# A transformer stack in split fp32 on one Trainium2 core: order of the latent fronts, the network rows, the first tiles and the mixed layer's entry, two bank placements, and bias reads spread over eight weight units

## The chip, the cores and the metric

The kernel runs on one core of one Trainium2 chip. The metric is the device time of one execution in microseconds (us), lower is better. Engines are called by the profile's names: PE (TensorE; PEld its weight loads), DVE (VectorE), ACT (ScalarE), POOL (GpSimd) and SP (SyncE, which here only issues DMAs). PSUM is eight banks of 128 partitions by 512 fp32 numbers.

## The reference, cut to what matters

512 tokens of width 1024 go through a first block of four layers (latent attention "mla", windowed attention "swa", forget-gate attention "fox", and mla again), and then through a second block of one layer with four mixers, a gated feed-forward network and a gated addition:

```python
for i in range(4):                       # mla, swa, fox, mla
    y = branch_i(x)
    x = layernorm(8 ** 0.25 * x + y, ln_g[i], ln_b[i])

def mla(x):                              # each branch ends with w_out
    cq, ckv, k_rope, gate = split(x @ w_in, 384, 256, 32, 1024)
    q = rmsnorm(cq) @ w_q_up             # 16 heads of 64 + 32 rotated
    k, v = split(rmsnorm(ckv) @ w_kv_up)
    return (causal_attention(q, k, v) * silu(gate)) @ w_out

h = rmsnorm(x); z = h @ w_in_2           # the second block, once
mix = concat(conv(z), pool(z), topk_attention(z, rel_bias), block_attention(z, rel_bias))
x = x + rmsnorm(mix @ w_out_2)
g, u = split(rmsnorm(x) @ w_gate_up)     # 2 x 2816 columns
x = x + rmsnorm((silu(g) * u) @ w_down)
x = x + sigmoid(rmsnorm(x) @ w_ple_gate) * (p @ w_ple_proj)
```

## The kernel before

**Weights.** Everything is a matrix product in split fp32: each operand is a high and a low part, and a product is three matmuls (`three`, lines 471 to 473). All weights pass in `units` of at most 128x1024 numbers (512 KB) in one fixed order (`plan_units`). For unit u, SP reads it into `w_raw` (ring of 3, line 1258) once the low part of unit u-3 is made; ACT copies it to `w_hi` (`split`, line 1277; ring of 4, so it also waits until PE has done with unit u-4); POOL subtracts to make `w_lo` (line 2604); PE waits for that in `unit`. ACT issues the splits at fixed places of its own program: `advance` splits the unit three ahead, and `early` pulls that next split forward to an earlier place.

**Products.** A `tile` is one unit of 128 columns against all 512 tokens: 8 steps of three matmuls, 24 in all, into one bank. Groups of results go in turn to banks 6 and 7; `begin` waits until the group before last of the same parity and all older ones have been drained (`bank_free`), unless the dictionary `place` names another bank, in which case it waits for nothing. `open_half` runs a unit against token columns 256 to 511 alone (24 matmuls of half the width) and leaves the group open for a later `tile` to finish; the third and fourth half opened at a time go to banks 4 and 5. `groups_stored(eng, n)` waits for all groups up to n.

**Token tiles.** `ROWS` is (3, 2, 1, 0). To multiply by x it must lie transposed: `turn_tile` on PE (8 transposes, line 871, into banks 2t and 2t+1), `turned_tile` on ACT (two copies to XTh, line 1498) and `low` on DVE (two subtractions to XTl, line 2161).

**Start.** SP reads the identity, four token tiles (line 1232) and then weights; PE transposes tiles 0 to 3; ACT copies all eight halves and then splits three units; PE then runs four whole tiles `c`.

**Latent fronts.** `mla` (used twice, j = 0 and 1) computes five latent tiles `c`, the sums of their squares, a rotated key tile and two gate tiles. On ACT `root` takes the square root of each sum and five copies make the high parts (line 1618). On DVE `scaled` takes a reciprocal of 128x512 (line 2250), scales (line 2252), and `low_latent` makes the low parts (line 2257). The three latents of the queries use the first root, the two of keys and values the second. After both, DVE finishes the two gate tiles (`gate`, line 1953), whose tanh ACT makes at line 1341. PE goes on with `rope(0)`, `query(0)`, `keys(0)`, whose groups follow the gates in banks 6 and 7.

**Row products.** `out_rows` multiplies n units of rows into all eight banks, four token tiles at a time; the last four units are held and run tile by tile in the order `ROWS`, with transposes of finished tiles put in at places given by `TURNS`: (row index, unit index) to which turn. `chunk_at(k)` gives the group count that unit k's input needs. The two calls for w_down have none and wait for every group first. `rms_tail` on ACT and DVE is the norm behind it: ACT squares, DVE adds and norms (`h_norm`, line 2175), each tile in a chain between the two. `ple_early` then runs the units of w_ple_gate on the first two rows between the last turns. `layer_tail_normed` and `ln_tail(3)` do the same after the last mla layer, where `early_mixed` opens four halves (`ik` and three `iq`) before the last two turns.

**Mixed layer's entry.** The halves are closed; PE transposes the small matrix of index weights (line 1095) as a group of its own, runs a fourth `iq` tile, and then goes through six pairs of a score block (line 1113) and a `conv` tile. The bias tables of the relative attention come back from DRAM to `G` as 32 reads of 64 KB (`bias_rows`, line 1239), four per head; SP issues two heads' reads ahead of each of the weight reads of four units from the first `conv` unit on, the first after waiting for `xt_lo`, the low parts of all turned tiles.

## Time and profile before

| | us |
|---|---|
| median of 3 runs | 1819.64 |
| lowest, highest | 1814.38, 1822.32 |
| the profiled execution | 1813.09 |
| its span | 1811.1 |
| PE busy | 1700.9 |
| DVE busy | 770.4 |
| ACT busy | 771.1 |
| POOL busy | 606.6 |

The time between span and the execution's own time is 1.99 us. Busy times of PE count a matmul's modelled end, so neighbours overlap a little. The rows further down are lines of the timeline, with the start and the duration in us from the span's start, and in square brackets the engine's idle time before the line and what ended it; and lines of the table by windows, with PE's busy time, the granted share of its full clock (1.00 is 2.4 GHz, 0.50 is 1.2 GHz), the DMA share and GB/s.

### The profile page before, as it was taken

The numbers are of one execution on the slowest core, as the hardware profiler recorded it, in microseconds if no ns is written. First come the engines' busy times: TensorE is split into PE (matmuls) and PEld (weight loads), VectorE is DVE, ScalarE is ACT, GpSimd is POOL, SyncE is SP. The second block draws the span as 40 slices with busy tenths as digits, with TensorE's granted clock in tenths as the row PEclk, the third lists the DMA queues.
The fourth block names the chain that finished last, engine by engine and source line by source line (L and its number), as shares of the span: only waits on it lengthen the run. The fifth ranks groups of instructions, "written<-read, shape, count | busy, mean of one in ns | idle before, by whom it ended". The sixth has DMA issues, their size and how long they took to land.

```text
span 1811.1 us, 24157 instructions
## 1 busy us (share of the span) xinstructions
PE 1700.9 (94%) x9303; PEld 1371.5 (76%) x9303; DVE 770.4 (43%) x2029; ACT 771.1 (43%) x1565; POOL 606.6 (33%) x304
## 2 busy tenths in 40 slices
PE   7899999999999999999899997997899999999988
PEld 6677778777788787787677777776678888787776
DVE  1566627456344434354565534877423111000152
ACT  4455643456244444433455633325634232112242
POOL 4222223323243332242422233372225444344323
PEclk9999999999999999999999998998899999999999
DMA  6221134233453222152321146321133333233312
GB/s 159 60 45 45 59 128 133 78 69 66 144 147 82 71 59 71 47 184 65 69 49 52 48 147 175 82 75 53 48 128 105 93 100 98 93 94 94 115 48 82
DMA packets 215693, 161.16 MB, mean 89 GB/s; under 512 B 53723, under 2 KB 196859, under 8 KB 215580
## 3 DMA queue, kind: packets, MB, share of 16 engines
q1 hardware_dynamic: 205616, 130.21, 25.6%
q10 hardware_dynamic: 9660, 29.12, 5.1%
q8 instruction: 75, 1.23, 0.3%
q0 software_dynamic: 304, 0.29, 0.2%
q14 instruction: 38, 0.31, 0.1%
HBM read 148.32 MB, written 11.14 MB: 88 GB/s over the span
## 4 chain that ended last, share of the span: by engine, by line
PE 61%; DVE 9%; ACT 5%; POOL 2%; DMA 2%; issue 2%; ACTq 1%; SPq 0%; POOLq 0%; DVEq 0%
PE banks L471 17%; PE banks L473 16%; PE banks L472 16%; PE banks L713 3%; PE banks L728 3%; PE banks L682 3%; POOL w_lo L2604 2%; ACT AB L1408 1%; ACT w_hi L1277 1%; DVE misc L2451 1%; DVE misc L2438 1%; PE banks L871 1%; DVE top L2450 1%; DVE AB L2101 1%; DVE QKl L1916 1%
## 5 line engine op out<-in xcount | busy, mean ns | idle before, releaser
L2604 POOL TENSOR_TENSOR w_lo<-w_raw,w_hi 128x1024 fp32r<-128x1024 f32 (+4 forms) x254 | 578.0, 2282 | 1174.9 <-ACT w_hi L1277 1174.6
L471 PE MATMUL banks<-XTh,w_hi 128*128 128x512 f32 (+3 forms) x1184 | 448.2, 379 | 23.3 <-POOL w_lo L2604 7.5
L473 PE MATMUL banks<-XTh,w_lo 128*128 128x512 f32 (+3 forms) x1184 | 441.8, 373 | 0.0
L472 PE MATMUL banks<-XTl,w_hi 128*128 128x512 f32 (+3 forms) x1184 | 441.5, 373 | 0.0
L1277 ACT ACTIVATE w_hi<-w_raw 128x1024 fp32r<-128x1024 f32 (+4 forms) x254 | 254.0, 1006 | 170.8 <-PE banks L473 90.7
L471 PEld LDWEIGHTS banks<-XTh,w_hi 128*128 128x128 f32 (+1 forms) x1184 | 224.0, 189 | 69.6 <-issue 22.0
L473 PEld LDWEIGHTS banks<-XTh,w_lo 128*128 128x128 f32 (+1 forms) x1184 | 223.8, 189 | 39.9
L472 PEld LDWEIGHTS banks<-XTl,w_hi 128*128 128x128 f32 (+1 forms) x1184 | 224.4, 190 | 38.3 <-issue 0.5
L471 PE MATMUL banks<-w_hi,OTh 128*128 128x512 f32 (+1 forms) x448 | 172.8, 386 | 6.8 <-POOL w_lo L2604 6.2
L473 PE MATMUL banks<-w_hi,OTl 128*128 128x512 f32 (+1 forms) x448 | 168.0, 375 | 0.0
L472 PE MATMUL banks<-w_lo,OTh 128*128 128x512 f32 (+1 forms) x448 | 167.8, 374 | 0.0
L1434 ACT ACTIVATE AB<-banks 128x512 f32<-128x512 f32 (+1 forms) x200 | 98.9, 528 | 147.3 <-PE banks L713 144.7
L1408 ACT ACTIVATE AB<-AB,nb 128x256 f32<-128x256 f32 (+3 forms) x288 | 152.9, 539 | 20.0 <-DVE nb L2082 17.1
L2529 DVE TENSOR_TENSOR otmp<-banks,AB 128x512 f32<-128x512 f32 x22 | 15.2, 692 | 280.9 <-PE banks L473 280.9
L2072 DVE CUSTOM_DVE_ANT_0 AB<-banks,zmask 128x384 f32<-128x384 f32 (+1 forms) x192 | 83.9, 487 | 102.1 <-PE banks L713 99.7
L2101 DVE TENSOR_SCALAR_CACHE_REDUCE AB<-AB,ri 128x256 f32<-128x256 f32 (+3 forms) x256 | 118.2, 518 | 2.3
L1916 DVE TENSOR_TENSOR QKl<-banks,QKh 128x512 fp32r<-128x512 f32 (+2 forms) x80 | 53.9, 682 | 135.4 <-ACT QKh L1307 134.2
L713 PE MATMUL banks<-ident,AB 128*128 128x128 f32 x672 | 98.0, 281 | 8.7 <-ACT AB L1434 5.9
L471 PEld LDWEIGHTS banks<-w_hi,OTh 128*128 128x128 f32 x448 | 84.3, 188 | 27.6 <-POOL w_lo L2604 8.3
L471 PE MATMUL banks<-w_hi,XTh 128*128 128x256 f32 (+2 forms) x288 | 90.7, 315 | 6.4 <-POOL w_lo L2604 5.6
L473 PEld LDWEIGHTS banks<-w_hi,OTl 128*128 128x128 f32 x448 | 84.3, 188 | 15.4
L713 PEld LDWEIGHTS banks<-ident,AB 128*128 128x128 f32 x672 | 73.7, 141 | 29.1 <-issue 17.5
(196 smaller groups left out, 2384.6 us busy)
## 6 DMA issues: line engine op xcount, KB each, us to landing
w_raw<-in_w_gate_up_dram SPq DMA_DIRECT2D x44, 512.0 KB, 3.8
w_raw<-in_fox_w_in_dram SPq DMA_DIRECT2D x30, 512.0 KB, 4.1
w_raw<-in_mla_w_in_dram SPq DMA_DIRECT2D x26, 512.0 KB, 4.1
w_raw<-in_w_in_dram SPq DMA_DIRECT2D x24, 512.0 KB, 3.8
w_raw<-in_w_down_dram SPq DMA_DIRECT2D x22, 512.0 KB, 3.5
w_raw<-in_swa_w_in_dram SPq DMA_DIRECT2D x20, 512.0 KB, 3.9
w_raw<-in_mla_w_out_dram SPq DMA_DIRECT2D x16, 512.0 KB, 3.6
x_spill<-AB ACTq DMA_DIRECT2D x16, 512.0 KB, 3.4
```

Source lines behind the costliest of these rows:

```text
L471: nc.tensor.matmul(o, ah, bh, start=first, stop=False, skip_group_check=True)
L472: nc.tensor.matmul(o, ah, bl, start=False, stop=False, skip_group_check=True)
L473: return nc.tensor.matmul(o, al, bh, start=False, stop=last, skip_group_check=True)
L682: mm = nc.tensor.matmul(bank[2 * (c.sch % 2) + x][:, cols], qp[r, pr.q, ts], kp[r, pr.k, ks], start=n == 0 and t == pr.s_chunks[ch][0], st ...
L713: mm = nc.tensor.transpose(bank[4 + c.tch % 2][:, o:o + P], SBP[a % 2][x][:, col:col + P], ident[:, :])
L1277: nc.scalar.activation(view(w_hi, u, RING), view(w_raw, u, RAW), ACT.Copy).then_inc(hi_done, 1)
L1408: ins = nc.scalar.activation(sc, sc, ACT.Exp, bias=nb[:, b, n0 + t:n0 + t + 1], scale=pr.scale, accum_out=rs[:, b, n0 + t:n0 + t + 1])
L1434: nc.scalar.activation(PTP[x][:, pr.pt[js[0]]:pr.pt[js[0]] + width], bank[4 + c.tch % 2][:, 0:width], ACT.Copy).then_inc(pt_free, 1)
L1916: return nc.vector.tensor_tensor(dst, src, h.bitcast(F32), ALU.subtract)
L2072: ins = nc.vector.tensor_tensor_reduce(pr.score(b, x, t), o, pr.bias(t, x), 1.0, -3e38, ALU.add, ALU.max, mx[:, b, 4 * x + t:4 * x + t + 1])
L2101: ins = nc.vector.tensor_scalar(pr.score(b, x, t), pr.score(b, x, t), ri[:, b, 4 * x + t:4 * x + t + 1], None, ALU.mult, ALU.add, accum_ou ...
L2604: pool.tensor_tensor(view(w_lo, u, RING), view(w_raw, u, RAW), view(w_hi, u, RING).bitcast(F32), ALU.subtract).then_inc(lo_done, 1)
```

## The change

It has these parts.

1. **First tiles.** SP reads token tiles 3 and 2, then two weight units, then token tiles 1 and 0, then the third unit. PE transposes tiles 3 and 2, opens the half of the first `c`, transposes tile 1, opens the second half, transposes tile 0, opens the third, and closes the three later. ACT copies tiles 3 and 2, splits unit 0, copies tile 1, splits unit 1, copies tile 0, splits unit 2. DVE follows in the same order.
2. **Latent fronts** (both mla layers). On ACT the high copies of the last two latents go behind the two gates' tanh. On DVE the first gate goes ahead of the second reciprocal and the second gate between it and the scaling.
3. **Network rows.** w_down's units wait each for its own group; the wait for all groups moves to the fourth token tile of the first unit. `TURNS["rms"]` turns the first finished tile one unit (six matmuls) later, in the two places where it is used, behind w_out_2 and behind w_down.
4. **Splits pulled forward.** In `rms_tail` `early()` goes between the last two copies; in `layer_tail_normed` ahead of the third and fourth deviation.
5. **Two groups in other banks.** The transposed index weights and the fourth `iq` tile go to banks 2 and 3, so that they wait for no `bank_free`.
6. **Bias reads.** One head's four reads go behind each of eight weight reads in place of eight ahead of each of four; the wait for `xt_lo` goes behind the first `conv` unit's read.

```diff
@@ -63,7 +63,7 @@
...
 ROWS = (3, 2, 1, 0)
-TURNS = {"ln": {(1, 3): 0, (2, 3): 1, (3, 3): 2}, "rms": {(2, 1): 0, (3, 1): 1}, "ln_rms": {(3, 1): 0, (3, 2): 1}}
+TURNS = {"ln": {(1, 3): 0, (2, 3): 1, (3, 3): 2}, "rms": {(2, 2): 0, (3, 1): 1}, "ln_rms": {(3, 1): 0, (3, 2): 1}}
 MLA_OUT = [5, 6, 7, 3, 4, 0, 1, 2]
@@ -809,7 +809,7 @@
...
                 paired = bool(begun)
-                if not begun:
+                if not begun and not chunk_at:
                     groups_stored(pe, c.g)
@@ -824,7 +824,7 @@
...
                             pe.wait_ge(pt_free, c.tch)
-                        if paired and k == 0 and t == T - 1:
+                        if (paired or chunk_at) and k == 0 and t == T - 1:
                             groups_stored(pe, c.g)
@@ -984,8 +984,18 @@
...
             pe.wait_ge(ident_in, 16)
-            for t in range(T):
-                turn_tile(t, lambda t: x_tok[:, t, :], (x_in[t], 16))
+
+            def turn_start(n):
+                turn_tile(ROWS[n], lambda t: x_tok[:, t, :], (x_in[ROWS[n]], 16))
+
+            turn_start(0)
+            turn_start(1)
+            pe.wait_ge(xt_lo, 4)
+            open_half("c")
+            turn_start(2)
+            open_half("c")
+            turn_start(3)
+            open_half("c")
             pe.wait_ge(xt_lo, c.xt)
@@ -1089,6 +1099,7 @@
...
                 tile("iq", n0=P)
+            place[c.g], place[c.g + 1] = 2, 3
             o = begin()
@@ -1169,13 +1180,15 @@
...
+            ff_at = []
             for lo, hi in ((0, KF_A), (KF_A, KF)):
...
                     tile("ff_up")
+                    ff_at.append(c.g)
                 out_rows("down", hi - lo, lambda k, ts: (ff_dst[lo + k][0][:, ff_dst[lo + k][2], ts],
                                                          ff_dst[lo + k][1][:, ff_dst[lo + k][2], ts]),
-                         first=lo == 0, last=lo > 0, turned=lambda t: HT[t % 2], turn_at=TURNS["rms"], early=ple_early)
+                         first=lo == 0, last=lo > 0, turned=lambda t: HT[t % 2], turn_at=TURNS["rms"], chunk_at=lambda k: ff_at[lo + k], early=ple_early)
                 if lo == 0:
@@ -1228,8 +1241,12 @@
...
             sp.dma_start(ident[:, :], consts["ident"]).then_inc(ident_in, 16)
-            for t in range(T):
+
+            def tokens(t):
                 sp.dma_start(x_tok[:, t, :], w["x"][0, t * P:(t + 1) * P, :]).then_inc(x_in[t], 16)
+
+            tokens(ROWS[0])
+            tokens(ROWS[1])
             conv0 = next(u for u, x in enumerate(units) if x[0] == "conv")
@@ -1241,12 +1258,9 @@
...
                     sp.wait_ge(lo_done, u - RAW + 1)
-                if u == conv0:
-                    sp.wait_ge(rel_dma, 16 * 8)
-                    sp.wait_ge(xt_lo, mark["mixed"])
-                if conv0 <= u < conv0 + 4:
-                    bias_rows(2 * (u - conv0))
-                    bias_rows(2 * (u - conv0) + 1)
+                if u == 2:
+                    tokens(ROWS[2])
+                    tokens(ROWS[3])
                 for k, c0, n, src in units[u][3]:
@@ -1256,6 +1270,11 @@
...
                     sp.dma_start(dst, src).then_inc(raw_in[u % RAW], 16)
+                if u == conv0:
+                    sp.wait_ge(rel_dma, 16 * 8)
+                    sp.wait_ge(xt_lo, mark["mixed"])
+                if conv0 <= u < conv0 + 8:
+                    bias_rows(u - conv0)
             for t in range(T):
@@ -1561,8 +1580,8 @@
...
                 turned_tile(ROWS[2])
+                early()
                 turned_tile(ROWS[3])
-                early()
@@ -1575,9 +1594,9 @@
...
                 advance(LEAD - 1)
+                early()
                 ln_deviation()
                 ln_deviation()
-                early()
                 x_squares(ROWS[2])
@@ -1613,12 +1632,18 @@
...
                     nc.scalar.activation(QKh[ROPE * n:ROPE * n + ROPE, 7, :], QKh[0:ROPE, 7, :].bitcast(F32), ACT.Copy).then_inc(kr_done, 1)
-                for i in range(5):
-                    act.wait_ge(c_tmp, 5 * j + i + 1)
-                    nc.scalar.activation(OTh[:, i, :], G[:, 2 + i, :], ACT.Copy).then_inc(c_hi, 1)
+
+                def high_latents(lo, hi):
+
+                    for i in range(lo, hi):
+                        act.wait_ge(c_tmp, 5 * j + i + 1)
+                        nc.scalar.activation(OTh[:, i, :], G[:, 2 + i, :], ACT.Copy).then_inc(c_hi, 1)
+
+                high_latents(0, 3)
                 for i in range(2):
...
                     gate(i)
+                high_latents(3, 5)
@@ -1674,10 +1699,10 @@
...
-            for t in range(T):
+            for n, t in enumerate(ROWS):
                 turned_tile(t)
-            for u in range(LEAD):
-                split(u)
+                if n:
+                    split(n - 1)
             act.wait_ge(pool_cst, 2)
@@ -2244,10 +2269,12 @@
...
+                def inverse_root(n, g):
+
+                    groups_stored(dve, g)
+                    link(nc.vector.reciprocal(DV[n], DV[n]))
+
                 def scaled(n, lo, hi):
-                    c.g += 1
-                    groups_stored(dve, c.g)
-                    link(nc.vector.reciprocal(DV[n], DV[n]))
                     for i in range(lo, hi):
@@ -2257,7 +2284,8 @@
...
                 hi_rope = {}
-                c.g += 4
+                c.g += 5
+                inverse_root(0, c.g)
                 scaled(0, 0, 3)
@@ -2268,12 +2296,16 @@
...
                     low_latent(i)
+                c.g += 1
+                root_at = c.g
+                gate(0)
+                gate_at[0] = c.g
+                inverse_root(1, root_at)
+                gate(1)
+                gate_at[1] = c.g
                 scaled(1, 3, 5)
...
                     low_latent(i)
-                for i in range(2):
-                    gate(i)
-                    gate_at[i] = c.g
@@ -2334,7 +2366,7 @@
...
-            for t in range(T):
+            for t in ROWS:
                 low(t)
```

What stands on ACT at the very start, before (copies to XTh and the first splits):

```order
1 L1498 ACT_TABLE_LOAD
2 L1498 ACTIVATE XTh<-banks 128x4x128 [waits xt_done] x8
3 L1277 ACTIVATE w_hi<-w_raw 128x1024 [waits raw_in0]
4 L1277 ACTIVATE w_hi<-w_raw 128x1024 [waits raw_in1]
5 L1277 ACTIVATE w_hi<-w_raw 128x1024 [waits raw_in2]
```

and after:

```order
1 L1517 ACT_TABLE_LOAD
2 L1517 ACTIVATE XTh<-banks 128x4x128 [waits xt_done] x4
3 L1296 ACTIVATE w_hi<-w_raw 128x1024 [waits raw_in0]
4 L1517 ACTIVATE XTh<-banks 128x4x128 [waits xt_done] x2
5 L1296 ACTIVATE w_hi<-w_raw 128x1024 [waits raw_in1]
6 L1517 ACTIVATE XTh<-banks 128x4x128 [waits xt_done] x2
7 L1296 ACTIVATE w_hi<-w_raw 128x1024 [waits raw_in2]
```

The splits of units 1 and 2 now stand behind copies that wait for PE's transposes of tiles 1 and 0 (`xt_done`), which PE runs behind the first and the second half tile.

On DVE in the first latent front, from the second reciprocal on, before:

```order
13 L2250 RECIPROCAL AB<-AB 128x512 [waits bank_free1,bank_free0]
14 L2252 SCALAR_TENSOR_TENSOR G<-G,qg,AB 128x512 [waits chain]
15 L2252 SCALAR_TENSOR_TENSOR G<-G,qg,AB 128x512
16 L2257 TENSOR_TENSOR OTl<-G,OTh 128x512 [waits c_hi] x2
17 L1953 SCALAR_TENSOR_TENSOR G<-G,banks 128x512 [waits g_hi,grp] x2
18 L1940 TENSOR_TENSOR AB<-banks,misc 128x512 [waits grp]
```

and after:

```order
13 L1978 SCALAR_TENSOR_TENSOR G<-G,banks 128x512 [waits g_hi,grp]
14 L2275 RECIPROCAL AB<-AB 128x512 [waits bank_free1,bank_free0]
15 L1978 SCALAR_TENSOR_TENSOR G<-G,banks 128x512 [waits g_hi,grp,chain]
16 L2279 SCALAR_TENSOR_TENSOR G<-G,qg,AB 128x512 x2
17 L2284 TENSOR_TENSOR OTl<-G,OTh 128x512 [waits c_hi] x2
18 L1965 TENSOR_TENSOR AB<-banks,misc 128x512 [waits grp]
```

The two gates (`G<-G,banks`), which free banks 6 and 7 for `rope(0)`, have moved ahead of the scaling of the last two latents.

On SP at the mixed layer's entry, before (the first row is the end of unit `ik`, the x4 are the four `iq` units):

```order
105 L1258 DMA w_raw<-in_w_in_dram 128x8x8
106 L1258 DMA w_raw<-in_w_in_dram 128x8x128 [waits lo_done] x4
107 L1239 DMA G<-rel_scratch 32x512 [waits xt_lo,rel_dma,lo_done]
108 L1239 DMA G<-rel_scratch 32x512 x7
109 L1258 DMA w_raw<-in_w_in_dram 128x8x128
110 L1239 DMA G<-rel_scratch 32x512 [waits lo_done]
111 L1239 DMA G<-rel_scratch 32x512 x7
112 L1258 DMA w_raw<-in_w_in_dram 128x8x128
```

and after:

```order
107 L1272 DMA w_raw<-in_w_in_dram 128x8x8
108 L1272 DMA w_raw<-in_w_in_dram 128x8x128 [waits lo_done] x5
109 L1256 DMA G<-rel_scratch 32x512 [waits xt_lo,rel_dma]
110 L1256 DMA G<-rel_scratch 32x512 x3
111 L1272 DMA w_raw<-in_w_in_dram 128x8x128 [waits lo_done]
112 L1256 DMA G<-rel_scratch 32x512 x4
113 L1272 DMA w_raw<-in_w_in_dram 128x8x128 [waits lo_done]
114 L1256 DMA G<-rel_scratch 32x512 x4
```

The first `conv` unit's read has moved ahead of the wait for `xt_lo`, and each later weight read has four bias reads ahead of it in place of eight.

## Rows read from the trace of the kernel before

**Rows 1.** Page, section 1: busy us (share of the span) xinstructions.

```profile
PE 1700.9 (94%) x9303; PEld 1371.5 (76%) x9303; DVE 770.4 (43%) x2029; ACT 771.1 (43%) x1565; POOL 606.6 (33%) x304
```

**Rows 2.** Timeline of PE at the start: start, us, operation, [idle before <-releaser].

```profile
17.55 0.77 PE L471 MATMUL banks<-XTh,w_hi 128*128 128x512 f32 x1 [4.30 <-POOL w_lo L2604]
...
41.39 0.39 PE L473 MATMUL banks<-XTh,w_lo 128*128 128x512 f32 x1
41.62 1.45 PE L885 MATMUL banks<-AB,ones 128*128 128x512 f32 x3
```

**Rows 3.** Timelines of ACT and POOL at the start.

```profile
10.37 0.60 ACT L1498 ACTIVATE XTh<-banks 128x512 fp32r<-128x512 f32 x1 [0.26 <-PE banks L871]
...
13.84 1.07 ACT L1277 ACTIVATE w_hi<-w_raw 128x1024 fp32r<-128x1024 f32 x1
...
22.89 2.39 POOL L2604 TENSOR_TENSOR w_lo<-w_raw,w_hi 128x1024 fp32r<-128x1024 f32 x1 [0.83 <-ACT w_hi L1277]
```

**Rows 4.** Windows of PE: stretch and length, busy, granted clock, DMA share, GB/s.

```profile
22.00:23.00 1.00, 1.00 (x5) 0.85 1.06 265
...
76.00:77.00 1.00, 1.00 (x4) 0.54 0.74 148
...
1544.00:1545.00 1.00, 1.00 (x6) 0.82 0.00 0
...
1547.00:1548.00 1.00, 1.00 (x4) 0.50 0.83 193
```

**Rows 5.** Timeline of PE in the two latent fronts.

```profile
72.19 0.77 PE L471 MATMUL banks<-OTh,w_hi 128*128 128x512 f32 x1 [4.09 <-DVE G L1953]
...
83.51 0.50 PE L471 MATMUL banks<-OTh,w_hi 128*128 128x512 f32 x1 [1.38 <-DVE QKl L1916]
...
863.30 0.76 PE L471 MATMUL banks<-OTh,w_hi 128*128 128x512 f32 x1 [4.09 <-DVE G L1953]
```

**Rows 6.** Timelines of DVE and ACT in the first latent front.

```profile
63.47 3.35 DVE L2250 RECIPROCAL AB<-AB 128x512 f32<-128x512 f32 x1
...
71.36 0.69 DVE L1953 SCALAR_TENSOR_TENSOR G<-G,banks 128x512 f32<-128x512 f32 x1 [1.71 <-ACT G L1341]
...
69.36 1.28 ACT L1341 ACT_TABLE_LOAD   x1
```

**Rows 7.** Timeline of PE at the mixed layer's entry.

```profile
1099.79 0.39 PE L471 MATMUL banks<-XTh,w_hi 128*128 128x256 f32 x1 [3.19 <-POOL w_lo L2604]
...
1108.08 0.34 PE L471 MATMUL banks<-XTh,w_hi 128*72 128x256 f32 x1 [1.90 <-DVE XTl L2161]
...
1124.04 0.66 PE L471 MATMUL banks<-XTh,w_hi 128*128 128x384 f32 x1 [4.66 <-DVE QKl L1916]
```

**Rows 8.** Timelines of SP, ACT and DVE at the mixed layer's entry.

```profile
1112.34 0.43 SPq L1258 DMA_DIRECT2D w_raw<-in_w_in_dram  x1
1112.81 3.82 SPq L1239 DMA_DIRECT2D G<-rel_scratch  x8
...
1121.43 1.06 ACT L1277 ACTIVATE w_hi<-w_raw 128x1024 fp32r<-128x1024 f32 x1 [3.39 <-DMA w_raw<-in_w_in_dram]
...
1098.97 1.85 DVE L2175 SCALAR_TENSOR_TENSOR AB<-AB,inv,V 128x1024 f32<-128x1024 f32 x1
...
1100.93 1.28 DVE L2175 SCALAR_TENSOR_TENSOR AB<-AB,inv,V 128x1024 f32<-128x1024 f32 x1
```

**Rows 9.** Timeline of PE at the first matmul of either w_down call.

```profile
1543.52 0.50 PE L471 MATMUL banks<-w_hi,QKh 128*128 128x512 f32 x1 [2.17 <-DVE OTl L1916]
...
1701.41 0.61 PE L471 MATMUL banks<-w_hi,QKh 128*128 128x512 f32 x1 [2.17 <-DVE QKl L1916]
```

**Rows 10.** Timelines of PE and POOL behind w_down.

```profile
1729.62 1.09 PE L871 MATMUL banks<-ident,AB 128*128 128x128 f32 x8 [1.83 <-DVE AB L2175]
...
1753.91 0.79 PE L471 MATMUL banks<-w_hi,XTh 128*128 128x512 f32 x1 [4.10 <-POOL w_lo L2604]
...
1751.51 2.34 POOL L2604 TENSOR_TENSOR w_lo<-w_raw,w_hi 128x1024 fp32r<-128x1024 f32 x1 [6.81 <-ACT w_hi L1277]
```

## The prediction

> **What bounds the kernel now.** I read the page first: PE is busy 94% of the span and no other engine over 43% [rows 1], so a time saved elsewhere counts only where PE waits for it. The second view is PE's own timeline, for its idle times of over half a us and what ended each: they sum to about 95 us, and the changed places hold the longest of them. The third is the windows, for the clock that PE was granted behind such a wait. There every wait of 2.2 us or more at a changed place costs twice: PE restarts at 72.19 and is at 1.2 GHz until about 76.9 (0.54 granted in 76 to 77), which loses half of 4.7 us, 2.35 us; at the start it is low from 17.55 to about 22.3 [rows 2, 4, 5]. Even the 2.17 us ahead of w_down bring 3.4 us of 1.2 GHz (1544.6 to 1548.0), a loss of 1.7 us [rows 4, 9]. Waits of 1.83 and 1.90 us brought none.
>
> **Latent fronts.** PE waits 4.09 us in either for DVE's gate, which stands behind a reciprocal of 3.35 us and the latents [rows 5, 6]. I rebuilt the first front in the new order, with the durations of the same rows. ACT ends the third high copy at 62.0; a split (0.5), the table load (1.28) and tanh (0.6) end at 64.4, since PE's first gate tile is done at 62.4. DVE's gate takes 0.69, to 65.2; the reciprocal ends at 68.5; the second gate, whose tanh waits for PE until 68.0, ends at 69.4; two scalings and two low parts end at 72.1. PE goes from the second gate (68.0) straight into `rope(0)`, whose second half needs a bank freed at 69.4, when PE arrives at 70.2. Next late is DVE's rotation behind the latents: its first operation frees the bank of `query(0)` at 72.9 (0.7 us of waiting), and the query's low part lets the second `keys` group start at 77.8 (1.5 us). That group started at 83.51 [rows 5]. So 5.7 us a front, of which 2.35 is clock; twice, **-11.4 us**. If nothing else than the 4.09 went, it would be -8.2; with a clock that falls anyway at the short waits, -6.7.
>
> **First tiles.** This is where I expect a loss. ACT's copies of tiles 3 and 2 end at 10.97, the split (1.06) at 12.0, and POOL's 2.39 lets PE start its first half tile at 14.6, 3 us sooner than 17.55 [rows 2, 3]. I assume unit 0 has landed by 11 because it is the third transfer in place of the fifth; no row shows it, and the bounds are 11 and 13.8, where its split started before. But then ACT stands at its copy of tile 1, PE transposes that only behind the half tile, and the split of unit 1 is behind the copy. Each further half tile therefore pays a whole chain in series: transposes 1.04 us, then copy, split and POOL. The chain behind the transposes is in the trace once in just this form, behind w_down: 4.10 us of idle PE, ended by POOL's low part [rows 10]. So a round is 5.14 us and a half tile. A half tile is 24 matmuls; a full-width one takes 0.23 us [rows 2], a half-width one half of that, estimated 0.12 us at 2.4 GHz and 0.21 at 1.2, so 2.9 or 5.1 us. After 4.1 us of idle the clock was low for over 4.5 us each time, so I take 5.0. From 14.6: half to 19.6, round to 24.7, half to 29.7, round to 34.9, half to 39.9. Then three closing halves (72 x 0.12 = 8.7) and the fourth tile (24 x 0.23 = 5.4) end at 54.0. Before, they ended at 41.62 [rows 2]. **+12.4 us**. With halves at full clock it is +6.0; with unit 0 at 13.8 it is 2.8 more than either. Nothing hides this: ACT, POOL and PE are all in the chain. The token reads of tiles 1 and 0 go past two weight reads on SP's queue, which costs nothing here, since PE asks for tile 1 only at 19.6.
>
> **Mixed layer's entry.** Three edits meet. (a) The fourth half's split waited on ACT behind two deviations; its POOL part ended at 1099.74 and PE waited 3.19 us [rows 7]. Pulled forward it can run at 1089.1, when its read lands (issued 1085.2, 3.9 us), and POOL is through at 1095.1, ahead of PE at 1096.6. PE then waits for DVE's `h_norm` at 1100.3 and 1101.9 instead, and the turned tiles are ready at 1104.9 in place of 1108.08, **-3.2**. (b) The fourth `iq` tile waited 4.66 us until 1124.04 for a bank, behind ACT, which stood for weights (3.39 us) that SP had issued behind eight bias reads of 3.82 us [rows 7, 8]. With bank 3 it needs only its own unit, ready at 1113.6, so it follows PE's work at 1116.5: 7.5 us sooner, of which 3.2 is (a), **-4.3**. It also ran at 1.2 GHz, 6.35 us where 384 columns at full rate take an estimated 4.1: **-2.2**. What comes next is late no longer: the first `conv` read issues at 1092.8, the second behind 1.9 us of bias reads at 1107, and a split that waits for one ends ahead of PE's need. The 32 bias reads end later, within the six `conv` tiles, and DVE asks for them only behind the two `pool` tiles that follow. Together **-9.7**, bounds -5 (clock not regained, second `conv` read late) and -11.
>
> One duration here is a matter of who else runs: DVE's `h_norm` took 1.85 us at 1098.97 while POOL was at its subtraction until 1099.74, and 1.28 us right behind [rows 8]. With the split pulled forward POOL is idle then, and I counted 1.28. The Trainium skill (SBUF — State Buffer, "SBUF: two separate sides") says that a DVE operation with two SBUF inputs and a GpSimd operation that reads SBUF exclude each other for a whole instruction. By that rule the 0.57 us come back, as counted; without it (a) would be -2.6.
>
> **Network rows.** The 2.17 us ahead of each w_down call go, since the first three token tiles need no fresh bank and PE reaches the fourth 4.1 us later. With the clock of 1.7 us: 3.9 each, **-7.7** (idle alone -4.3). The added waits join matmuls that already wait for their weights. Turning one unit later moves six matmuls (1.4 us) into the 1.83 us wait at 1729.62 [rows 10], but the next transposes wait for `h_norm` again, and the tile after that is held by DVE until 1742.3 as before; behind w_out_2 likewise. I count **0**, at most -1.
>
> **Splits pulled forward, w_ple_gate.** The fourth unit's split goes ahead of ACT's last copy: 1747.45, POOL ends at 1750.95 where it ended at 1753.85 [rows 10]. PE waits 1.1 in place of 4.10 us, -2.9; it also ran slow until about 1759.7, which loses 2.8. **-5.7**, idle alone -2.9. Pulling it forward behind w_out_2 is hidden by later work: 0.
>
> **The sum**: -11.4 + 12.4 - 9.7 - 7.7 - 5.7 = -22.1 us. Against the profiled execution's 1813.09 that is 1791.0. That execution is 6.6 us below the median of the runs, so for a median I take 1819.64 - 22.1 = 1797.5.
>
> **Rivals.** (A) The start is at full clock in its half tiles: +6.0, total -28.5, 1791. For it: at w_down the clock fell only a us behind the restart [rows 4, 9]. Against: it was low at 17.55 after the same idle. (B) The start gains as its order suggests, 3 us, because reads and splits overlap somehow: -37.5, 1782. Against it stands the order on ACT. (C) The gains lose their clock share: the short waits that stay (0.7 and 1.5; 0.7, 0.6 and 1.9; 1.1) add up and hold the clock low as before. Then the gains are 6.7 + 7.5 + 4.3 + 2.9 = 21.4 and the total is -9.0, 1811. (D) Slower: as (C), and at the start the clock never returns between rounds nor in the closing 96 matmuls. The transposes double (2 x 1.0), the closing halves and the fourth tile double (8.7 + 5.4): +28.5 in place of +12.4, total +7, 1827. It decides where more than 16 us of extra low clock come at the start. Against it: the clock returned behind every restart after 4 to 6 us of work. (E) The fronts gain little, since DVE's later latents delay `keys`: then each front gives 2, total -14.7, 1805.
>
> **How the numbers follow.** The forecast 0.50, (A) 0.17, (B) 0.05, (C) 0.09, (D) 0.04, (E) 0.15. The forecast's own range is 1790 to 1804. The range to hold eight in ten reaches over (A) and (E), and takes some of the runs' own spread (1814 to 1822): 1785 to 1808. A measurement of this kernel can tell 0.5%, 9.1 us, from no change. Faster by more: the forecast, (A), (B), (E), and a little less for the spread, 0.87. Within: most of (C), half of (D), 0.10. Slower: 0.03.
>
> **What would show it.** PE's first `c` matmul near 14.6, then two idle times of about 4 us ended by POOL's low part at about 25 and 35, and the sum of squares (128x512 of `ones`) starting near 54 in place of 41.62. No 4.09 us idle in the fronts, and the first `keys` groups about 6 us nearer to the gates. The 384-column matmuls following PE's small transposes without a wait and at six a us. No 2.17 us at w_down. One idle of about 1 us behind the last transposes of w_down. I am wrong if PE waits less than 2 us in the start's rounds, or if the stretch from 1100 to 1131 keeps its length, which would say that another engine holds it.

## The result and the profile after

The changed kernel takes 1790.47 us (median of 4 runs, 1789.03 to 1791.87) where the kernel before took 1820.90 us beside it (median of 4, 1814.38 to 1822.32): ratio 0.9851, 95% interval 0.9831 to 0.9871 (the ratio is not the quotient of the two medians, which is 0.9833). The two profiled executions are 1813.09 and 1790.19 us, 22.9 us apart; the sum of the prediction was 22.1.

Page of the changed kernel, section 1 (answers to [rows 1]): PE has 72 matmuls more, since three full tiles became six half tiles, and is busy 8.9 us less. That fits a mean granted clock of 0.986 in place of 0.977: less of its work runs at 1.2 GHz.

```profile
PE 1692.0 (95%) x9375; PEld 1369.1 (77%) x9375; DVE 770.8 (43%) x2029; ACT 770.7 (43%) x1565; POOL 607.8 (34%) x304
```

Timeline of PE at the start of the changed kernel (answers to [rows 2]; the last value is the idle time before, with what ended it):

```profile
14.98 0.55 PE L471 MATMUL banks<-XTh,w_hi 128*128 128x256 f32 x1 [4.61 <-POOL w_lo L2636]
...
19.41 1.04 PE L871 MATMUL banks<-ident,AB 128*128 128x128 f32 x8
...
24.55 0.39 PE L471 MATMUL banks<-XTh,w_hi 128*128 128x256 f32 x1 [4.10 <-POOL w_lo L2636]
...
29.02 1.03 PE L871 MATMUL banks<-ident,AB 128*128 128x128 f32 x8
...
34.15 0.39 PE L471 MATMUL banks<-XTh,w_hi 128*128 128x256 f32 x1 [4.10 <-POOL w_lo L2636]
...
52.70 2.73 PE L885 MATMUL banks<-AB,ones 128*128 128x512 f32 x6
```

PE starts 2.6 us sooner (14.98 for 17.55) and has finished four tiles 11.1 us later (52.70 for 41.62). In between it stands twice for 4.10 us, and the timeline of ACT shows why:

```profile
11.29 1.06 ACT L1296 ACTIVATE w_hi<-w_raw 128x1024 fp32r<-128x1024 f32 x1 [0.29 <-DMA w_raw<-in_mla_w_in_dram]
20.05 1.08 ACT L1517 ACTIVATE XTh<-banks 128x512 fp32r<-128x512 f32 x2 [7.70 <-PE banks L871]
21.02 1.06 ACT L1296 ACTIVATE w_hi<-w_raw 128x1024 fp32r<-128x1024 f32 x1
```

ACT is idle for 7.70 us in front of a copy that waits for PE's transposes, and the split of the next unit, which needs nothing from PE, stands behind it.

Timeline of PE in the two latent fronts of the changed kernel (answers to [rows 5]):

```profile
84.14 0.47 PE L471 MATMUL banks<-OTh,w_hi 128*128 128x512 f32 x1 [0.84 <-DVE AB L1965]
88.64 0.50 PE L471 MATMUL banks<-OTh,w_hi 128*128 128x512 f32 x1 [0.84 <-DVE QKl L1941]
...
872.16 0.47 PE L471 MATMUL banks<-OTh,w_hi 128*128 128x512 f32 x1 [0.85 <-DVE AB L1965]
876.60 0.50 PE L471 MATMUL banks<-OTh,w_hi 128*128 128x512 f32 x1 [0.74 <-DVE QKl L1941]
```

The idle time of 4.09 us is gone. From the end of the second gate tile to the first `keys` group it was 83.51 - 67.94 = 15.57 us; now it is 88.64 - 79.05 = 9.59. In the second front it was 15.88 and is 9.52.

Timeline of PE at the mixed layer's entry of the changed kernel (answers to [rows 7]):

```profile
1099.04 1.09 PE L871 MATMUL banks<-ident,AB 128*128 128x128 f32 x8 [0.84 <-DVE AB L2200]
1100.68 1.09 PE L871 MATMUL banks<-ident,AB 128*128 128x128 f32 x8 [0.54 <-DVE AB L2200]
...
1103.34 0.34 PE L471 MATMUL banks<-XTh,w_hi 128*72 128x256 f32 x1 [1.57 <-DVE XTl L2186]
...
1116.12 0.44 PE L471 MATMUL banks<-XTh,w_hi 128*128 128x384 f32 x1
```

The waits of 3.19 and 4.66 us are gone, and three short ones (0.84, 0.54, 1.57) have taken the place of the first. Behind them the clock fell, as the window shows (stretch and length, busy, granted clock, DMA share, GB/s):

```profile
1104.00:1105.00 1.00, 1.00 (x7) 0.50 0.42 90
...
1116.00:1117.00 1.00, 1.00 (x8) 1.00 1.10 309
```

At w_down neither call has an idle time ahead of it, and windows 1532 to 1533 and 1686 to 1687 have a granted clock of 1.00. Behind the second w_down (answers to [rows 10]):

```profile
1712.42 1.09 PE L871 MATMUL banks<-ident,AB 128*128 128x128 f32 x8 [0.47 <-DVE AB L2200]
1718.24 1.09 PE L871 MATMUL banks<-ident,AB 128*128 128x128 f32 x8 [0.61 <-DVE AB L2200]
...
1733.66 0.53 PE L471 MATMUL banks<-w_hi,XTh 128*128 128x512 f32 x1 [1.07 <-POOL w_lo L2636]
```

1.83 us has become 0.47 and 0.61, and 4.10 us at w_ple_gate has become 1.07. One wait has grown: the first w_out_2 matmul, POOL's in either kernel, waited 1.18 us at 1342.10 before and waits 2.26 now.

```profile
1333.08 0.50 PE L471 MATMUL banks<-w_hi,OTh 128*128 128x512 f32 x1 [2.26 <-POOL w_lo L2636]
```

How far the changed kernel is ahead of (-) or behind the kernel before, from the starts of the same matmuls in both timelines of PE:

| place | before | after | difference |
|---|---|---|---|
| first sum of squares | 41.62 | 52.70 | +11.08 |
| `keys`, first front | 83.51 | 88.64 | +5.13 |
| end of the second gate tile, second front | 859.05 | 867.08 | +8.03 |
| `keys`, second front | 874.93 | 876.60 | +1.67 |
| first `ik` half | 1087.81 | 1086.54 | -1.27 |
| `idx` | 1131.63 | 1122.02 | -9.61 |
| w_out_2 | 1342.10 | 1333.08 | -9.02 |
| behind the first w_down | 1633.67 | 1620.53 | -13.14 |
| third turned tile behind the second w_down | 1742.37 | 1725.13 | -17.24 |
| span | 1811.1 | 1788.1 | -23.0 |

Between the fronts nothing was edited, and the changed kernel loses 2.9 us there and wins as much back between the second front and the entry. The last section comes to that.

### The profile page after: what moved, and what is told of

Read it like the earlier page. It is cut to its first block, busy times and chain, and to the rows that moved or that the text cites. A ratio compares the mean times of both kernels' runs of the same rounds, so it can differ in the third digit from the quotient of the medians.

```text
span 1788.1 us, 24318 instructions
## 1 busy us (share of the span) xinstructions
PE 1692.0 (95%) x9375; PEld 1369.1 (77%) x9375; DVE 770.8 (43%) x2029; ACT 770.7 (43%) x1565; POOL 607.8 (34%) x304
## 4 chain that ended last, share of the span: by engine, by line
PE 60%; DVE 10%; ACT 5%; POOL 2%; DMA 2%; issue 2%; ACTq 1%; POOLq 0%; DVEq 0%
PE banks L471 17%; PE banks L472 16%; PE banks L473 16%; PE banks L713 3%; PE banks L728 3%; PE banks L682 3%; POOL w_lo L2636 2%; ACT AB L1427 1%; ACT w_hi L1296 1%; DVE misc L2483 1%; DVE top L2482 1%; ACT G L1547 1%; DVE misc L2470 1%; DVE AB L2126 1%; PE banks L871 1%
## 5 line engine op out<-in xcount | busy, mean ns | idle before, releaser
L471 PE MATMUL banks<-XTh,w_hi 128*128 128x512 f32 (+4 forms) x1208 | 454.2, 376 | 23.7 <-POOL w_lo L2636 12.8
L472 PE MATMUL banks<-XTl,w_hi 128*128 128x512 f32 (+4 forms) x1208 | 447.3, 370 | 0.0
L473 PE MATMUL banks<-XTh,w_lo 128*128 128x512 f32 (+4 forms) x1208 | 446.9, 370 | 0.0
L471 PEld LDWEIGHTS banks<-XTh,w_hi 128*128 128x128 f32 (+1 forms) x1208 | 230.1, 190 | 69.9 <-issue 17.8
L473 PEld LDWEIGHTS banks<-XTh,w_lo 128*128 128x128 f32 (+1 forms) x1208 | 230.2, 191 | 39.1
L472 PEld LDWEIGHTS banks<-XTl,w_hi 128*128 128x128 f32 (+1 forms) x1208 | 230.4, 191 | 37.0 <-issue 0.5
L471 PEld LDWEIGHTS banks<-w_hi,OTh 128*128 128x128 f32 x448 | 84.2, 188 | 28.7 <-POOL w_lo L2636 10.9
L472 PEld LDWEIGHTS banks<-w_lo,OTh 128*128 128x128 f32 x448 | 84.4, 188 | 13.8
```

Of the source, the lines that this page charges most:

```text
L471: nc.tensor.matmul(o, ah, bh, start=first, stop=False, skip_group_check=True)
L472: nc.tensor.matmul(o, ah, bl, start=False, stop=False, skip_group_check=True)
L473: return nc.tensor.matmul(o, al, bh, start=False, stop=last, skip_group_check=True)
```

## The experiments

The theory: PE's work is nearly one unbroken row, so each edit shifts all that follows by its own amount, and the amounts add; the start alone costs, through ACT's order. The rivals: gains are absorbed further on, the start is slow for another reason, or the edits at the entry cure one and the same wait.

Each kernel was compared with the kernel before on the same chip; all together it ran 62 times there, with a median of 1815.15 us (1808.99 to 1822.66). Gains in us below are the ratio's distance from 1, times 1815; an interval in us is that of the ratio.

### The start alone, and undone

```diff
+            turn_start(0)
+            turn_start(1)
+            pe.wait_ge(xt_lo, 4)
+            open_half("c")
+            turn_start(2)
...
+            for n, t in enumerate(ROWS):
+                turned_tile(t)
+                if n:
+                    split(n - 1)
```

These lines, with the order of the token reads, were put alone into the kernel before (`only_start`) and taken out of the changed kernel (`undo_start`).

> The kernel before with nothing changed but the order of the first tiles. Theory: first ones matmul at 52.7 us, time 11.1 us above the kernel before (1.006 of it), since the shift is carried rigidly to the end. Rival (absorbed later): within 3 us of the kernel before.

> The changed kernel with the first tiles as they were before it (four token tiles transposed and copied in a row, then the three splits, four full c tiles). Theory (the start costs its whole shift, since PE is at work nearly without a break behind it): the first ones matmul goes from 52.7 back to 41.6 us and the time from 1790.5 to 1779.4, 0.977 of the kernel before. Rival (the time lost at the start is absorbed later, as PE then finds weights and latents ready): within 3 us of 1790.5.

Measured: alone 1.0044 (1.0028 to 1.0060), 8.0 us slower, with an interval of 5.1 to 10.9 that just misses the 11.1. Undone: 0.9808 (0.9777 to 0.9839) of the kernel before, where the changed kernel has 0.9851 and, measured again below, 0.9870: 8 to 11 us faster than it. The forecast 0.977 lies just outside its interval. So most of the shift is carried to the end, and the rival of a loss within 3 us is out. In the trace of `only_start` the sum of squares begins at 53.01, 11.4 us behind the 41.62 of before:

```profile
24.21 0.39 PE L471 MATMUL banks<-XTh,w_hi 128*128 128x256 f32 x1 [4.10 <-POOL w_lo L2621]
...
53.01 2.74 PE L885 MATMUL banks<-AB,ones 128*128 128x512 f32 x6
```

Two things make the loss smaller than 11.1. The first is the yardstick: nine traces have the old start, and in them the sum of squares begins at 41.62 to 43.29 (median 42.70). The trace of before is the earliest of the nine, so against a usual execution the 53.01 are 10.3 us late; in `undo_start` it begins at 43.10, and not at the forecast 41.6. The second is that part of it comes back as clock: over its ten runs the span times (1 - granted clock) has a median of 39.2 us, against 41.7 for the kernel before. One place shows it. Behind the same 4.08 us wait of the first front, `keys` follows 10.48 us later (83.58 to 94.06), in the kernel before 11.32 (72.19 to 83.51), 0.84 us more.

### The cause of the start's loss

```diff
-            for n, t in enumerate(ROWS):
-                turned_tile(t)
-                if n:
-                    split(n - 1)
+            turned_tile(ROWS[0])
+            turned_tile(ROWS[1])
+            for u in range(LEAD):
+                split(u)
+            turned_tile(ROWS[2])
+            turned_tile(ROWS[3])
```

> The changed kernel, only that ACT splits units 0, 1 and 2 ahead of its copies of token tiles 1 and 0; the half tiles stay. Theory (the loss is the chain of transposes, ACT copy, ACT split and POOL low part run in series once a half tile): POOL's low parts end at about 15, 17 and 20 us, the two idle times of 4.1 us go, PE runs 15.0 to 41.5 with the first ones matmul at about 41.5, time 11 us below the changed kernel, 1779.5. Rival (the loss is in the half tiles, which run at 1.2 GHz, and in token reads that land late): two idle times of 2 us or more stay and the time gains under 5 us.

Measured 0.9791 (0.9760 to 0.9822). Timeline of PE in `splits_first`:

```profile
14.55 0.55 PE L471 MATMUL banks<-XTh,w_hi 128*128 128x256 f32 x1 [4.57 <-POOL w_lo L2638]
...
19.18 1.04 PE L871 MATMUL banks<-ident,AB 128*128 128x128 f32 x8
...
22.93 1.04 PE L871 MATMUL banks<-ident,AB 128*128 128x128 f32 x8
...
40.78 2.74 PE L885 MATMUL banks<-AB,ones 128*128 128x512 f32 x6
```

Only ACT's order differs, and both waits of 4.10 us are gone; the sum of squares begins 11.9 us sooner than in the changed kernel (40.78, forecast 41.5), while the first half tile is as slow as there (14.55 to 19.18, 4.63 us). The serial chain is the cause. The half tiles themselves are not, nor the later token reads.

### A start that beats both

The four tiles are transposed first, unit 0 is split between ACT's copies of tiles 2 and 1, tokens 1 and 0 are read ahead of unit 1, and one tile is opened by half.

```diff
+            turned_tile(ROWS[0])
+            turned_tile(ROWS[1])
+            split(0)
+            turned_tile(ROWS[2])
+            turned_tile(ROWS[3])
+            for u in range(1, LEAD):
+                split(u)
```

> The changed kernel with all four token tiles transposed first, reads in the order x3, x2, unit 0, x1, x0, unit 1; ACT splits unit 0 between its copies of tiles 2 and 1, the rest behind them; only the first c tile is opened by half. Theory: first c matmul at 15.0 us as in the changed kernel, no idle time over 1 us behind it, first ones matmul at about 39 us, time 13.5 us below the changed kernel, 1777, so some 2.5 us below the one with the start undone. Rival (units 1 and 2 land or are split too late for PE, since the reads of two token tiles and unit 0 share the queues): idle time ahead of the second c tile, and no gain against the start undone.

Measured 1775.01 us, 0.9770 (0.9746 to 0.9795): faster than the kernel before by 42 us and than the changed kernel by some 15 us, as its interval lies wholly below both of that kernel's. Timeline of PE:

```profile
12.84 3.67 PE L871 MATMUL banks<-ident,AB 128*128 128x128 f32 x16 [2.83 <-DMA AB<-in_x_dram]
38.77 2.73 PE L885 MATMUL banks<-AB,ones 128*128 128x512 f32 x6
```

The forecast 39 was met, but not its first step. The tokens landed at 12.84, so the first `c` matmul came only behind the transposes, at 16.2 and not at 15.0. But then it had no wait ahead of it, and from its fifth matmul on the half tile ran at full pace (0.12 us from one to the next): it took 2.89 us, where half a tile had taken 4.43 us in the changed kernel. PE did restart slowly behind its wait of 2.83 us, but the slow stretch fell on the transposes: 16 of them took 3.33 us, 0.21 us each, where 8 take 0.79 us in `splits_first` (19.18 to 19.97).

### The fronts alone

The edit is the DVE and ACT part of the diff: the gates ahead of the later latents.

> The kernel before with only the new order of the two latent fronts. Theory (each front is a rigid gain of the 4.09 us idle time and of the slow clock behind it, less short new waits): from the end of the second gate tile to the first keys group 9.6 us in place of 15.6 in either front, time 12 us below the kernel before (0.9934 of it). Rival (half of the gain belongs to the other edits, or the later latents and queries give it back further on in the layer): under 6 us.

Measured 0.9910 (0.9885 to 0.9935), 16.3 us, interval 11.8 to 20.9. Timeline of PE:

```profile
74.69 0.47 PE L471 MATMUL banks<-OTh,w_hi 128*128 128x512 f32 x1 [0.84 <-DVE AB L1946]
79.19 0.50 PE L471 MATMUL banks<-OTh,w_hi 128*128 128x512 f32 x1 [0.82 <-DVE QKl L1922]
```

The second gate tile ends at 69.61, so it is 9.58 us to `keys`, and 9.6 was expected. The rival is out: nothing is given back. The mean lies 4 us above the trace's 12.3 us, and the six runs have a granted clock of 0.979 to 0.985 where the kernel before has a median of 0.977. Which later places keep their clock because of the fronts was not settled.

### The network rows alone

```diff
-                if not begun:
+                if not begun and not chunk_at:
...
-                        if paired and k == 0 and t == T - 1:
+                        if (paired or chunk_at) and k == 0 and t == T - 1:
```

> The kernel before with only the waits of w_down bound to each chunk and the later turn behind w_down. Theory: both idle times of 2.17 us ahead of w_down go, with the slow clock behind them, 3.9 us each, and the turn gives nothing; time 7.8 us below the kernel before (0.9957 of it). Rival (the last chunk's low part then holds the matmuls further on, or the clock falls all the same): 4 us or less.

Measured 0.9965 (0.9942 to 0.9988), 6.4 us, interval 2.2 to 10.5. Neither w_down call has an idle time ahead of it. The traced execution as a whole is no shorter than that of before (span 1811.2 against 1811.1 us; its clock of 0.974 is the lowest of the nine): it is 7.4 us behind at w_out_2 already, ahead of every edit of this run. From there the two w_down places win 8.1 us back. The later turn did as forecast (timeline of PE in `only_network`):

```profile
1729.83 1.09 PE L871 MATMUL banks<-ident,AB 128*128 128x128 f32 x8 [0.47 <-DVE AB L2177]
1735.65 1.09 PE L871 MATMUL banks<-ident,AB 128*128 128x128 f32 x8 [0.62 <-DVE AB L2177]
...
1742.55 1.09 PE L871 MATMUL banks<-ident,AB 128*128 128x128 f32 x8
...
1754.11 0.79 PE L471 MATMUL banks<-w_hi,XTh 128*128 128x512 f32 x1 [4.10 <-POOL w_lo L2606]
```

The first turned tile runs to 1742.55 in 12.72 us, as in the kernel before (1729.62 to 1742.37, 12.75), so the later turn is worth nothing. The 4.10 us wait stays where the split isn't moved.

### The split pulled forward in rms_tail alone

```diff
-                turned_tile(ROWS[3])
                 early()
+                turned_tile(ROWS[3])
```

> The kernel before with only the split pulled ahead of ACT's last copy in rms_tail. Theory: the 4.10 us idle time at w_ple_gate becomes 1.1 us and the slow clock behind it goes, 5.7 us from there to the end; nothing changes behind w_out_2. Rival (the clock stays low behind the shorter wait too, since two other short ones stand shortly ahead of it): 3 us.

Measured 0.9986 (0.9965 to 1.0007), 2.5 us with an interval from a loss of 1.3 to a gain of 6.4: the runs alone can't tell the forecast 5.7 from the rival's 3 or from nothing. The trace shows the wait changed as expected:

```profile
1754.67 1.03 PE L871 MATMUL banks<-ident,AB 128*128 128x128 f32 x8
1756.78 0.50 PE L471 MATMUL banks<-w_hi,XTh 128*128 128x512 f32 x1 [1.08 <-POOL w_lo L2604]
```

Its eighteen matmuls begin with 0.50 us in place of 0.79: the clock is full. From the third turned tile (1748.26) to the end of the span it is 63.0 us, in the kernel before 68.7: 5.7 us, as forecast, in this one execution.

### The mixed layer's entry, whole and in parts

```diff
+                early()
                 ln_deviation()
                 ln_deviation()
-                early()
...
+            place[c.g], place[c.g + 1] = 2, 3
...
-                if conv0 <= u < conv0 + 4:
-                    bias_rows(2 * (u - conv0))
-                    bias_rows(2 * (u - conv0) + 1)
+                if conv0 <= u < conv0 + 8:
+                    bias_rows(u - conv0)
```

> The kernel before with only the three edits at the mixed layer's entry (split pulled forward, two groups in banks 2 and 3, bias reads spread). Theory: from the first ik half to the idx tile 34.0 us in place of 43.8, with three short idle times left ahead of the rest of ik; time 8 to 10 us below the kernel before (0.995 of it). Rival (the stretch keeps part of its length because the conv and pool weights now come later): under 5 us, and longer idle times in the conv and pool tiles.

> The kernel before with only the fourth half's split pulled forward at the mixed layer's entry. Theory (three causes in a row: split, bank, bias reads): the 3.19 us idle time goes, the rest of ik starts 3.2 to 3.5 us sooner, SP's wait for the turned tiles is met as much sooner and so the first conv weight too, so the fourth iq tile still waits about 4.7 us for its bank but all of it 3 us sooner; time 3 us below the kernel before. Rival (the weight issue does not move): the fourth iq tile waits 8 us and the time stays.

> The kernel before with only the two groups in banks 2 and 3. Theory: the 3.19 us idle time stays; the fourth iq tile no longer waits for ACT (which still stands at a weight behind eight bias reads) and its 4.66 us idle time goes with the slow clock behind it, 6 us; time 5 to 6.5 us below the kernel before. Rival (ACT's late copies hold the next group instead): the idle time moves to the idx tile or the first conv tile, under 2 us.

> The kernel before with only the bias reads spread over eight units and the first conv weight read ahead of them. Theory: the weight at which ACT stood for 3.39 us lands some 5 us sooner, so the bank is free in time without the other banks; the 3.19 us idle time stays, the 4.66 us one goes or falls under 1 us; gain the same 5 to 6.5 us as with the banks alone, which would make the two edits two cures of one wait. Rival (the bank is late by DVE's own work): at least 3 us of idle time stay at the fourth iq tile.

Starts in us from the first `ik` half, out of each kernel's timeline of PE; the last column is a matmul that waits 4.88 us for DVE in every kernel, 100 us further on:

| kernel | rest of ik | fourth iq | idx | later marker | ratio (interval) |
|---|---|---|---|---|---|
| before | 20.27 | 36.23 | 43.82 | 144.56 | 1 |
| split early | 16.80 | 33.01 | 41.19 | 140.33 | 0.9976 (0.9953 to 0.9998) |
| banks | 18.76 | 29.99 | 39.48 | 142.36 | 0.9998 (0.9979 to 1.0017) |
| bias reads | 20.25 | 32.96 | 40.19 | 139.35 | 0.9983 (0.9971 to 0.9994) |
| all three | 16.80 | 29.58 | 35.37 | 136.09 | 0.9938 (0.9917 to 0.9959) |

The three together meet the forecast: 8.5 us in the trace, 11.3 in the runs (7.4 to 15.1). The split pulled forward meets its 3 us (2.6 at `idx`, 4.4 in the runs with an interval of 0.4 to 8.5). The other two hold the surprise. The banks were expected to bring 5 to 6.5 us and bring 0.4 in the runs, at most 3.8 by the interval. Timelines of PE and ACT in `entry_banks`:

```profile
1124.26 0.44 PE L471 MATMUL banks<-XTh,w_hi 128*128 128x384 f32 x1
...
1133.75 0.58 PE L1114 MATMUL banks<-QKh 64*128 64x256 f32 x2 [5.05 <-DVE QKl L1917]
```

```profile
1131.60 1.06 ACT L1278 ACTIVATE w_hi<-w_raw 128x1024 fp32r<-128x1024 f32 x1 [3.51 <-DMA w_raw<-in_w_in_dram]
1132.57 0.47 ACT L1308 ACTIVATE QKh<-banks 128x384 fp32r<-128x384 f32 x1
```

The fourth `iq` tile no longer waits, but ACT still stands 3.51 us at a weight, so its copy of that tile comes at 1132.57, and the `idx` tile behind it waits 5.05 us in place of 1.24. That is the rival of this expectation. The 2.2 us that the marker shows are for the most part the clock, which happened not to fall behind the 3.20 us wait this time (the third half then takes 2.98 us in place of 4.42). The marker flatters two other rows by such a chance too: between `idx` and the marker `entry_early` and `entry_bias` run 1.6 us quicker than before (99.1 and 99.2 us for 100.7), since their clock stayed up behind a wait of 3.0 us near 1182 where it fell in before. The column `idx` is the better measure for them: 2.6 and 3.6 us. With the bias reads spread (timeline of ACT in `entry_bias`), ACT has no such wait, and the tile waits 1.41 us:

```profile
1119.45 1.05 ACT L1276 ACTIVATE w_hi<-w_raw 128x1024 fp32r<-128x1024 f32 x1
1121.53 0.49 ACT L1306 ACTIVATE QKh<-banks 128x384 fp32r<-128x384 f32 x1 [1.03 <-PE banks L473]
1121.92 1.05 ACT L1276 ACTIVATE w_hi<-w_raw 128x1024 fp32r<-128x1024 f32 x1
```

So the eight bias reads ahead of a weight made most of the wait, 3.25 of 4.66 us, and the bank alone only hid it from one tile. The gain is smaller than the forecast 5 to 6.5 us: 3.6 at `idx`, 3.1 in the runs (1.1 to 5.3), for 1.41 us of wait stay and the clock fell behind them. The three together win 8.5 us at `idx`, the split and the bias reads alone 2.6 and 3.6: the missing 2.2 us fit the 1.41 us wait and its clock, which the bank would then save once ACT no longer stands at a weight. No run has those two edits without the banks, so this is not shown.

`h_norm` gives the prediction's argument on shared access a test. In `entry_bias` POOL subtracts from 1102.46 to 1104.81, and in `entry_early` it has ended by 1097.77 (timelines of DVE, `entry_bias` and then `entry_early`):

```profile
1104.06 1.84 DVE L2174 SCALAR_TENSOR_TENSOR AB<-AB,inv,V 128x1024 f32<-128x1024 f32 x1
```

```profile
1101.66 1.28 DVE L2175 SCALAR_TENSOR_TENSOR AB<-AB,inv,V 128x1024 f32<-128x1024 f32 x1
```

0.56 us, as the prediction counted. The trace agrees in kind with the exclusion that the Trainium skill states (SBUF — State Buffer, "SBUF: two separate sides"): another DVE operation of this shape, with one of its inputs in a bank of PSUM, took 1.28 us in `entry_bias` at 1102.67, fully beside the same subtraction. The size does not fit exactly: the two overlap by 0.75 us (1104.06 to 1104.81), 0.2 us more than `h_norm` lost.

### The changed kernel again

No edit.

> The changed kernel again, beside many runs of the kernel before on this chip. Theory (the edits are worth 23 to 26 us, and the median of before in the first comparison, 1820.9 us of four runs, was high by chance of the clock): 1789 us, 26 us below before's 1815.2, and less than the 30.4 us first found. Rival (the full 30.4 us are real and the profiled execution of before was a fast exception): 1785 us.

Measured 1794.17 us (1784.85 to 1794.56), 21.5 below the 1815.67 of the kernel before on that chip, ratio 0.9870 (0.9841 to 0.9899). The rival of 30.4 us is out, and the forecast 26 was too high by 4.5 us of medians. The first comparison's 30.4 us was helped by a high median of before, as supposed; the edits are worth 22 to 27 us.

## Why the prediction was right

The time, 1790.5, lies 7.0 us under the predicted 1797.5 and within its range; on the second chip 1794.2. Taken alone it would fit rival (A) as well, which said 1791. What decides between them is the trace: like is compared with like there, and the predicted 1791.0 for a profiled execution stands beside 1790.19 (by (A) it would be 1784.6), and the half tiles took 4.43 and 4.47 us where (A) has 2.9. By its steps, with the places of the trace between the profiled executions and the runs of each edit alone:

| term | predicted | trace | edit alone (interval) |
|---|---|---|---|
| latent fronts | -11.4 | -12.3 | -16.3 (-20.9 to -11.8) |
| first tiles | +12.4 | +11.1 | +8.0 (+5.1 to +10.9) |
| mixed entry | -9.7 | -8.3 | -11.3 (-15.1 to -7.4) |
| network rows | -7.7 | -8.2 | -6.4 (-10.5 to -2.2) |
| w_ple_gate | -5.7 | -5.8 | -2.5 (-6.4 to +1.3) |
| w_out_2 | 0 | +0.6 | - |
| sum | -22.1 | -22.9 | -28.5 |

The product of the five single ratios is 0.9843, beside 0.9851 and 0.9870 for all edits at once: within their intervals, of 3 to 5 us each way for every edit, they add, as a row of rigid shifts does. That the sum of the trace comes so near is in part luck, as misses of +1.4 and +0.6 us stand against -1.3, -0.9, -0.5 and -0.1, and the drift of 2.9 us between the fronts was won back behind them.

**Latent fronts.** Right in each step: the clock share came back, since the waits that stay are 0.84 and 0.84 (0.7 and 1.5 were forecast). Rival (E) is out.

**First tiles.** The mechanism is as forecast, to the 4.10 us of each round and a start at 14.98 (14.6). The weight of which the prediction had no row was there in time: ACT split it at 11.29, after a wait of 0.29 us. The size that was off is the half tile: 4.43 us (14.98 to 19.41) and 4.47 (24.55 to 29.02) against 5.0. In the first the pace was back after 3.3 us; I had carried over more than 4.5. Between (A), at 2.9, and the forecast, the truth is nearer to the forecast.

**Mixed entry.** The total missed 1.4 us, because rival (C) came true in this one place: behind the waits of 0.84, 0.54 and 1.57 us the `ik` and `iq` rest ran at 1.2 GHz for about 3 us (0.50 in the window shown), 1.5 us of loss. It is a matter of chance: seven traces have these three waits, and the clock fell behind them in three (`after`, `after_again`, `only_entry`) and held in four. The waits came as forecast. What the prediction had wrong was whose gain it is: it gave 4.3 us and 2.2 us of clock to the bank. By the experiments the bank alone brings none of it, and the bias reads alone bring 3.6 us.

**Network rows, the turn, w_ple_gate.** Right in place and, by the traces, in size: no wait at w_down, 0 for the turn, 1.07 us left of 4.10. The runs alone don't tell the 5.7 us of w_ple_gate from nothing.

**w_out_2.** This was not in the sum. The wait grew by 1.08 us, which moves the place by 0.6, since shorter waits just ahead of it went. It belongs to none of the edits. Over the 14 traces it is 1.18 to 2.37 us: 1.20 in `only_entry`, but 2.14 in `only_start` and 1.80 in `only_network`, which have no edit between the fronts and this place. In each the chain is the same, ACT at the transfer of the weight, then its split and POOL's subtraction. What makes the transfer late in some executions is open.

**The base.** The sum was subtracted from a median of three runs, 1819.64. The 62 later runs have 1815.15, and 1815.15 - 22.1 = 1793.0 stands between the two medians of the changed kernel. So that step made the larger part of the 7.0 us, 4.5, and no term of the sum missed by over 1.4 us.

## What to carry over

In each engine's order, look for an instruction that needs nothing from the bottleneck engine but stands behind one that waits for it: half a tile's head start was bought with a chain run in series three times, and moving three splits back ahead of the copies recovered 12 us at that place. Before a buffer is changed to cure a wait, follow the wait back through the engine that fills it; if that engine stands at a transfer, the wait only moves one tile on. And where all but one engine have slack, count what each idle time of the bound engine costs in clock as well, and test single edits by the trace and not only by time, since half a per cent is as large as the spread. Hold a place against the same place in several traces, since unedited places differ too (41.62 to 43.29 at the old start, 1.18 to 2.37 us of wait at w_out_2).

## What the runs showed of the hardware

The spread of one kernel's runs goes with its clock. Over the 62 runs of the kernel before, the granted clock goes from 0.973 to 0.983 and the time from 1822.66 to 1808.99, with a correlation of -0.87. Even with the same instructions and the same wait, it falls or it doesn't. Four `rope` groups in each of 14 traces wait 2.21 to 2.24 us for DVE; behind 37 of these 56 the clock fell to 0.5 and behind 19 it stayed. Timelines of PE in `splits_first` and `new_start`, and then a window of each just behind:

```profile
138.29 0.47 PE L471 MATMUL banks<-OTh,w_hi 128*128 128x512 f32 x1 [2.24 <-DVE AB L1967]
```

```profile
136.31 0.53 PE L471 MATMUL banks<-OTh,w_hi 128*128 128x512 f32 x1 [2.21 <-DVE AB L1964]
```

```profile
139.00:140.00 1.00, 1.00 (x6) 1.00 0.10 25
```

```profile
137.00:138.00 1.00, 1.00 (x4) 0.50 0.09 22
```

From there to the next such group it is 40.31 us in the first and 41.47 in the second. Over the 28 such stretches those without a fall take 40.27 to 40.32 us and those with one 40.78 to 41.49: a fall costs 0.5 to 1.2 us. This is also the drift of 2.9 us between untouched places in the table of the result: the clock of the changed kernel fell at 192, 332 and 342, where the one before kept it, and held at 938 and 979, where the one before lost it.

The start shows another side. PE was slow behind either restart, 3.3 us in the changed kernel (14.98 to 18.32) and 4.3 us in `new_start` (12.84 to 17.15), although the windows' granted clock says 1.00 throughout. Windows of PE in the changed kernel, both with nothing but matmuls of 256 columns (five, then ten in a us, counting those that reach in from before):

```profile
15.00:16.00 1.00, 1.00 (x5) 1.00 1.07 286
...
18.40:19.40 1.00, 1.00 (x10) 1.00 0.02 7
```

So at the very start the spacing of the matmuls, 0.21 us at first and 0.12 from 18.3 on, tells the pace, and the clock column doesn't.
